# Bouncing two mixer outputs through DRAM: smaller pieces, another order, and residual rows on GpSimd's queue

## The reference, cut to what matters

```python
z = _rms_norm(h, norm_mix_g)
p = z @ w_in                                  # [conv value | conv gate | S5 input], 512 channels each
conv_out = silu(_layer_norm(conv31(conv_v * sigmoid(conv_gate)) + conv_b))
y = s5_forward(ssm_u) + s5_backward(ssm_u) + d_skip * ssm_u
y = gelu(y)
ssm_out = y * sigmoid(y @ glu_w + glu_b)
h = h + concat(conv_out, ssm_out) @ w_out     # 1024 x 1024
z = _rms_norm(h, norm_ffn_g)
h = h + square(relu(z @ w_ff1)) @ w_ff2       # 1024 -> 4096 -> 1024
out = _rms_norm(h, norm_final_g)
```

## Time and profile before

| | us |
|---|---|
| three runs of the kernel | 924.2, 924.34, 1046.33 |
| median | 924.34 |
| the profiled execution, its own time | 924.33 |
| its span on the slowest core (core 0) | 923.3 |
| spans of the eight cores | 917.6 to 923.3 |
| mean granted TensorE clock of the cores | 0.945 to 0.953 |

### The profile page before, as it was taken

How to read it: one execution, slowest core, us unless ns; L and a number is a source line. 1 busy time by engine, 2 the same in 40 slices (tenths; PEclk the granted TensorE clock), 3 DMA queues, 4 the chain that set the end, 5 groups by cost and what they waited for, 6 DMA issues and landing times.

```text
span 923.3 us, 15660 instructions; the slowest of 8 cores (917.6 to 923.3 us)
## 1 busy us (share of the span) xinstructions
PE 777.3 (84%) x4515; PEld 388.4 (42%) x4584; DVE 497.0 (54%) x955; ACT 367.6 (40%) x596; POOL 400.2 (43%) x454
## 2 busy tenths in 40 slices
PE   0466667598886996689999999999999999999992
PEld 0233334246344565235544444444444444444440
DVE  5647971847878845426643343343343343343487
ACT  5878976534124455636632112111111111111453
POOL 3777991864879816000043323324333333323220
PEclk9978888799998999879999999999999999999997
DMA  8469974561449885699041410606023060510134
GB/s 229 149 201 241 168 183 81 94 99 33 66 79 103 75 129 154 181 229 262 6 60 33 65 28 2 91 1 92 1 38 55 1 92 1 70 22 1 46 137 182
DMA packets 71955, 87.27 MB, mean 95 GB/s; under 512 B 7584, under 2 KB 55840, under 8 KB 71872
## 3 DMA queue, kind: packets, MB, share of 16 engines
q1 hardware_dynamic: 56752, 66.18, 30.8%
q0 software_dynamic: 14400, 19.76, 14.3%
q10 hardware_dynamic: 720, 0.33, 0.1%
HBM read 86.56 MB, written 19.45 MB: 115 GB/s over the span
## 4 chain that ended last, share of the span: by engine, by line
PE 66%; DVE 8%; issue 8%; ACT 7%; DMA 5%; SPq 3%; POOL 2%; DVEq 0%; ACTq 0%; POOLq 0%
PE p_pb L1142 24%; PE p_pb L1162 23%; PE p_pb L1088 6%; SPq L162 3%; PE p_pb L1011 3%; DVE p_pb L477 2%; PE p_pb L448 2%; ACT s_zt L349 2%; DMA scr_uc<-s_usc 2%; DMA s_xt<-xl 2%; PE p_pb L691 1%; PE p_pb L930 1%; ACT s_wb L640 1%; DVE s_vo L477 1%; PE p_pb L941 1%
## 5 line engine op out<-in xcount | busy, mean ns | idle before, releaser
L477 DVE TENSOR_TENSOR s_h<-s_h,p_pb 128x512 f32<-128x512 f32 x288 | 197.7, 687 | 262.2 <-PE p_pb L1162 246.6
L477 POOL TENSOR_TENSOR s_hid<-s_rl 128x512 bf16<-128x512 f32 x128 | 133.7, 1049 | 322.8 <-ACT s_rl L1150 308.3
L1162 PE MATMUL p_pb<-s_w2c,s_hid 128*128 128x512 bf16 x1005 | 225.7, 379 | 5.1 <-DVE s_h L477 4.1
L1142 PE MATMUL p_pb<-s_zf,s_w1c 128*128 128x512 bf16 x1002 | 224.9, 379 | 1.2
L1150 ACT ACTIVATE s_rl<-p_pb 128x512 f32<-128x512 f32 x128 | 76.1, 597 | 327.7 <-PE p_pb L1142 315.4
L1162 PEld LDWEIGHTS p_pb<-s_w2c,s_hid 128*128 128x128 bf16 x1024 | 99.4, 98 | 126.5 <-issue 7.9
L1142 PEld LDWEIGHTS p_pb<-s_zf,s_w1c 128*128 128x128 bf16 x1024 | 100.2, 98 | 120.0
L448 PE MATMUL p_pb<-s_zsl,s_winu 128*128 128x512 bf16 x243 | 72.1, 447 | 11.6 <-ACT s_ust L462 9.2
L372 PE MATMUL p_pb<-s_ident,s_zt 128*128 128x128 bf16 (+1 forms) x264 | 24.7, 249 | 45.3 <-ACT s_zt L358 34.7
L842 PE MATMUL p_pb<-s_zsl,s_winv 128*128 128x512 bf16 x250 | 55.6, 379 | 5.5 <-DVE s_usc L858 3.8
L448 PEld LDWEIGHTS p_pb<-s_zsl,s_winu 128*128 128x128 bf16 x256 | 27.2, 112 | 44.7 <-issue 28.2
(11 more groups left out here) (168 smaller groups left out, 940.2 us busy)
## 6 DMA issues: line engine op xcount, KB each, us to landing
s_xt<-xl SPq DMA_DIRECT2D x32, 512.0 KB, 6.1
s_h<-xl SPq DMA_DIRECT2D x16, 512.0 KB, 17.5
s_w1c<-w_ff POOLq DMA_DIRECT2D x8, 1024.0 KB, 9.9
s_w2c<-w_ff POOLq DMA_DIRECT2D x8, 1024.0 KB, 10.5
out<-s_h SPq DMA_DIRECT2D x15, 512.0 KB, 2.6
s_wstv<-w_in SPq DMA_DIRECT2D x4, 1024.0 KB, 8.9
s_kf<-scr_rs SPq DMA_DIRECT2D x8, 384.0 KB, 18.6
s_wstu<-w_in SPq DMA_DIRECT2D x4, 512.0 KB, 10.9
```

Of the source, the lines that this page charges most:

```text
L477: op(eng, lambda e: e.tensor_tensor(o, a, b_, op=o_), r=r, w=w)
L1142: op("pe", lambda e, k=k, f=f: e.matmul(pb[pi_][:, :], w1c[fc % 2][:, k, f * 128:(f + 1) * 128], zf[:, k, b * 512:(b + 1) * 512], start=(k ...
L1162: op("pe", lambda e, f=f, half=half: e.matmul(pb[pi_][:, :], hid[hb][:, f, ti * 128:(ti + 1) * 128], w2c[fc % 2][:, f, half * 512:(half + ...
```

## The change

Three edits. (1) The state space part is written and read per call of `ssm_out`: `ys_write(i)` writes four groups (256 KB) in each of eight calls, and `ys_read(i)` reads them with four DMAs of 64 KB. In `ys_out(i)` the reads of piece i - 1 are issued before the write of piece i. `gs` has eight keys in place of four. (2) The convolution part goes by pairs of channel chunks, and lies in the scratch in the order in which it is read: `yc_write(j)` writes 16 groups with eight DMAs, one per time residue (16 partitions x 16 rows of 512 bytes, 128 KB each, 1 MB together), and `yc_read(c)` reads a chunk with one DMA (128 partitions x 4 KB, 512 KB). (3) `resid_load` is on GpSimd's queue.

```diff
-    def back_write(name, src, skey, c):
-
-        P.dma("sp", bass.AP(scr[name], c * 128 * 2048, [[256, 128], [128 * 256, 8], [1, 256]]), src[:, 8 * c:8 * c + 8, :],
-              r=[skey], w=["scr_%s%d" % (name, c)])
-
-    def back_read(name, c, dst, dkey):
-        for gl in range(8):
-            P.dma("sp", dst[16 * gl:16 * gl + 16, c, :].rearrange("p (t k) -> p t k", t=8),
-                  bass.AP(scr[name], c * 128 * 2048 + gl * 128 * 256, [[256, 16], [16 * 256, 8], [1, 256]]),
-                  r=["scr_%s%d" % (name, c)], w=["%s_%d" % (dkey, gl)])
+    def ys_write(i):
+
+        P.dma("sp", bass.AP(scr["ys"], 4 * i * 128 * 256, [[256, 128], [128 * 256, 4], [1, 256]]), gs[:, 4 * i:4 * i + 4, :],
+              r=["gs%d" % i], w=["scr_ys%d" % i])
+
+    def ys_read(i):
+        c = i // 2
+        for gl in range(4 * (i % 2), 4 * (i % 2) + 4):
+            P.dma("sp", mixs[16 * gl:16 * gl + 16, c, :].rearrange("p (t k) -> p t k", t=8),
+                  bass.AP(scr["ys"], (8 * c + gl) * 128 * 256, [[256, 16], [16 * 256, 8], [1, 256]]),
+                  r=["scr_ys%d" % i], w=["mixs%d_%d" % (c, gl)])
+
+    def yc_write(j):
+
+        for t in range(8):
+            P.dma("sp", bass.AP(scr["yc"], 16 * j * 16 * 2048 + 256 * t, [[2048, 16], [16 * 2048, 16], [1, 256]]),
+                  sil[16 * t:16 * t + 16, 16 * j:16 * j + 16, :], r=["sil%d" % (2 * j), "sil%d" % (2 * j + 1)], w=["scr_yc%d_%d" % (j, t)])
+
+    def yc_read(c):
+        P.dma("sp", mixc[:, c, :], bass.AP(scr["yc"], c * 128 * 2048, [[2048, 128], [1, 2048]]),
+              r=["scr_yc%d_%d" % (c // 2, t) for t in range(8)], w=["mixc%d" % c])
...
     def resid_load(t):
-        P.dma("sp", h[:, t, :], _rows(xl, 2 + 128 * (t % 2), t // 2), w=["h%d" % t])
+        P.dma("pool", h[:, t, :], _rows(xl, 2 + 128 * (t % 2), t // 2), w=["h%d" % t])
...
     def ys_out(i, banks):
         ssm_out(2 * i, banks, stk)
-        if i % 2 == 1:
-            c = i // 2
-            back_write("ys", gs, "gs%d" % c, c)
-            if c > 0:
-                back_read("ys", c - 1, mixs, "mixs%d" % (c - 1))
+        if i > 0:
+            ys_read(i - 1)
+        ys_write(i)
...
     def yc_out(c):
         for i in range(4 * c, 4 * c + 4):
             ln_silu(i)
-        back_write("yc", sil, "sil%d" % c, c)
-        if c > 0:
-            back_read("yc", c - 1, mixc, "mixc%d" % (c - 1))
+        if c % 2 == 1:
+            yc_write(c // 2)
+            yc_read(c - 1)
+            yc_read(c)
 
     for i in range(8):
         ys_out(i, (0, 1) if i % 2 == 0 else (6, 7))
-    back_read("ys", 3, mixs, "mixs3")
+    ys_read(7)
     for c in range(4):
         yc_out(c)
-    back_read("yc", 3, mixc, "mixc3")
```

More of the change, by code:

```diff
@@ L983, in ln_silu @@
         op("act", lambda e: e.activation(sil[:, 2 * i:2 * i + 2, :], yv[:, 2 * i:2 * i + 2, :], AF.Silu), r=["yv%d" % i], w=["sil%d" % (i // 4)])
-    def back_write(name, src, skey, c):
-        P.dma("sp", bass.AP(scr[name], c * 128 * 2048, [[256, 128], [128 * 256, 8], [1, 256]]), src[:, 8 * c:8 * c + 8, :],
-              r=[skey], w=["scr_%s%d" % (name, c)])
-    def back_read(name, c, dst, dkey):
-        for gl in range(8):
-            P.dma("sp", dst[16 * gl:16 * gl + 16, c, :].rearrange("p (t k) -> p t k", t=8),
-                  bass.AP(scr[name], c * 128 * 2048 + gl * 128 * 256, [[256, 16], [16 * 256, 8], [1, 256]]),
-                  r=["scr_%s%d" % (name, c)], w=["%s_%d" % (dkey, gl)])
+    def ys_write(i):
[14 more added lines that the diff above has]
+              r=["scr_yc%d_%d" % (c // 2, t) for t in range(8)], w=["mixc%d" % c])
     for c in range(4):
         for gl in range(8):
-            P.place("mixc%d_%d" % (c, gl), "mixc", WIN + 8192 + 4096 * c, 4096, 16 * gl, 16 * gl + 16)
+            P.place("mixc%d" % c, "mixc", WIN + 8192 + 4096 * c, 4096)
             P.place("mixs%d_%d" % (c, gl), "mixs", WB2 + 4096 * c, 4096, 16 * gl, 16 * gl + 16)
     gs = at("gs", [128, 32, 256], BF16, VV1)
-    for c in range(4):
-        P.place("gs%d" % c, "gs", VV1 + 4096 * c, 4096)
+    for i in range(8):
+        P.place("gs%d" % i, "gs", VV1 + 2048 * i, 2048)
     def ssm_out(pp0, banks, stk):
@@ L1039, in ssm_out @@
             op("act", lambda e, g0=g0, bi=bi: e.activation(gs[:, g0:g0 + 3:2, :], pb[bi][:].rearrange("p (g k) -> p g k", g=2), AF.Gelu_apprx_tanh),
-               r=[pbk[bi]], w=["gs%d" % (pp0 // 4)])
+               r=[pbk[bi]], w=["gs%d" % (pp0 // 2)])
     gluw = sb("gluw", [128, 4, 512], BF16, UST)
@@ L1045, in _build @@
     msk = [["mixs%d_%d" % (c, gl) for gl in range(8)] for c in range(4)]
-    mck = [["mixc%d_%d" % (c, gl) for gl in range(8)] for c in range(4)]
+    mck = [["mixc%d" % c] for c in range(4)]
     def glu_mm(b, banks):
@@ L1490, in _build @@
         resid_load(t)
-    P.dma("pool", w1c[0][:], w1v[:, :, 0:512], r=["mixc3_7"], w=["w1c0"])
+    P.dma("pool", w1c[0][:], w1v[:, :, 0:512], r=["mixc3"], w=["w1c0"])
     P.dma("pool", w2c[0][:], w2v[0], w=["w2c0"])
```

## The result

The ratio of the changed kernel to the one before is 1.0172, with a 95% interval of 1.0117 to 1.0227. On the 924.34 us of before that is 940.2; the forecast was 938. The ratio leaves out disturbed executions, which the plain medians of that comparison, 942.17 and 937.82, hold. So the kernel is slower; whether by more than 2% the interval leaves open. The profiled execution after took 940.96.

A forecast was written before the change was run, and what follows sets the result against it. SP's in-order DMA queue was taken to bound the stretch where TensorE waits for mixs and mixc. State space +12.9 and convolution with loads +1.6 gave 14.5, taken as 13.7 on 924.33: 938 us, range 927 to 946.

The forecast's parts named there:

- Part 2: Convolution part, 16 issues fewer but two landings in series: 20.7 us in place of 26.4, gaining 5.7 us alone.
- eight writes at 0.5 us: Convolution part, first eight writes on SP's queue: last issued at 3.5, landed at 6.2 us after SP is free.
- Part 1, the step: State space part, per piece on SP's queue: landing 2.7, wake-up 0.15, four reads 2.35, together 5.2 us; loss +12.9 us.
- the four reads at 4 x 0.59: State space part, SP's issue of one piece's four reads of mixs: 2.35 us of each step.
- The wake-up of 0.15: State space part, time from a write's landing to the first read's issue on SP's queue: 0.15 us.
- The GELU spacing: State space part: a GELU pair every 3.1 to 3.3 us, so SP falls behind from the second piece on.
- Part 1, the first write: State space part, first ys write beside the wout and gluw loads: 2.7 + 1.3 = 4.0 us, landed 344.7.
- Part 3: Residual loads on GpSimd's queue compete with the convolution part's DMAs: cost 7.3 us, turning -5.7 into +1.6.
- Sum: Whole kernel: 12.9 + 1.6 = 14.5 us, taken as 13.7 because some h loads start later than the reads; 938 us.
- Rival 1: Residual loads on GpSimd's queue don't disturb: +12.9 - 5.7 = +7.2, 931.5 us; chance 0.22.
- Rival 2: State space round trips longer: step 6 us, +18, and +2 for the rest, 944 us; over 943, chance 0.2.
- Rival 3: State space part keeps pace with the GELUs (step under 3.3 us): -2 to -9, about 918 us; chance 0.08.

The follow-up runs named there:

- e2: Only the convolution part's edit (pairs of chunks, row order) on the kernel before, residual loads still on SP's queue; ratio 0.9981, a gain of 1.8 us.
- e1: Only the state space part's edit (pieces of four groups, reads of piece i-1 before write i) on the kernel before; ratio 1.0105, 9.8 us slower.
- e4: Changed kernel with the write of piece i issued ahead of the reads of piece i-1 in the state space part; 1.001 of the kernel before.
- e3: Only the residual loads moved to GpSimd's queue, on the kernel before; ratio 1.0219, 20.3 us slower.
- e5: Changed kernel with the residual loads back on SP's queue; 1.0096 of the kernel before.
- e7: From e6, the eight writes of a pair in residue order 0, 1, 4, 5, 2, 3, 6, 7; 0.995 of the kernel before.
- e6: From e5, state space write ahead of the previous piece's reads, and all sixteen convolution writes ahead of the four reads; 0.9959 of the kernel before.
- e10: From e7, reads of the first pair issued after the fourth write of the second pair; 0.9958 of the kernel before.
- e9: From the kernel before, each residual load on GpSimd's queue moves a 1 KB quarter of the rows of four tiles; ratio 1.0311, last landing 429.0.

## Why the prediction was right or wrong, and which terms were off

The direction, the order of the writes as the main loss and the price of part 3 came out as forecast. The step that failed is the sum of part 2. That the total still came near is luck: two errors of opposite sign.

**Part 2, the step that failed.** "So the part alone gains 5.7 us"; measured by itself it gains 1.8. The term mis-sized most is "eight writes at 0.5 us", the last landed 6.2 after the start. In e2 the first read went out 8.6 us after the first write, and in the changed kernel, 384.03 to 393.03, 9.0. The 0.5 is the issue of a write of 512 KB from 128 partitions (two in 1.00 us); these are 128 KB from 16 partitions and keep SP 0.7 to 0.8 us each with nothing beside them. What holds them stays open. The last reads landed 5.9 us after their issue, where the sum had 4.8. That sum also has allowances that it doesn't name: 7.3 + 7.2 is given as 15.2, and 15.9 + 3.6 (1.05 MB at 290 GB/s) as 20.7.

**Part 1, the step.** Right in kind: shown by e1 and by the swap in e4. The step was forecast at 5.2 us and measured 4.75. Landing was 2.7 (median of the eight writes), as taken. The term that was too large is the four reads at 4 x 0.59: they take 1.72. The 0.59 was a mean over groups of eight and sixteen (0.74, 0.57 and 0.52); groups of four took 0.43 each in seven of eight cases. The wake-up of 0.15 was read from a gap between two issues that waited for nothing; it is too small to matter. The GELU spacing named with the earlier trace rows is 3.05 us there and 3.5 for the pair before it, not 3.1 to 3.3, and nothing hangs on that either.

**Part 1, the first write.** It failed on the other side. "Half of that excess for half the bytes" gave 4.0 us; it took 9.0. In the earlier trace rows the first write took 5.8 and in the changed kernel 9.0, yet both landed at about 348. The last of the two weight loads on GpSimd's queue landed at 346.4 before and at 348.4 after. That the write waited for their traffic is read from this, and from what the queues moved in the changed kernel from 339.5 to 348.7 us, four times as much on GpSimd's; no run moves those loads:

```profile
q0 software_dynamic: 799, 1.05, 74.6%
q1 hardware_dynamic: 528, 0.26, 12.8%
```

So issuing the write earlier gained nothing. The two errors cancelled: SP was free at 383.8 (forecast 383.6), the GLU got going at 386.06 (forecast 385.7). Alone, part 1 cost 9.8 us and not 12.9.

**Part 3.** Forecast +7.3 beside part 2; measured 7.0 beside parts 1 and 2 and 4.2 beside part 2 alone. So the size is right here. Where it falls is not: the prediction put 4.5 us on the stretch with h0 and h1 (15.2 to 19.7) and 2.8 on the last two reads, which were to share with h2 and on. The traces have about 5.0 on the first and nothing on the last reads (5.83 us against 5.92). Even shares also fail elsewhere: against the 64 KB reads with rows of 512 bytes the same loads cost 20.3 us (e3), where I had expected 2 to 8. The rule that the prediction weighed, of the Trainium skill, "DMA: Bandwidth & Descriptors", section "Issuing engines are not separate DMA queues", says that the queues interleave on the same DMA engines. The traces agree in that loads on GpSimd's queue held up SP's transfers; how unevenly they can share it doesn't say. Whether a second queue brings bandwidth isn't settled here: the prediction took 249 and 253 GB/s as equal, but e3 moved 333 with both.

**Sum.** 12.9 + 1.6 = 14.5, taken as 13.7; measured 1.72% = 15.9 us. By the single measurements it is 9.8 - 1.8 + 7.0 = 15.0: part 1 was put 3.1 us too high, the gain of part 2 3.9 us too high, and only because the two nearly cancel is the total close. Rival 1 (loads don't disturb) is refuted by e5, which is faster than the changed kernel and has 10.2 us where that has 15.2. Rival 2 (a step of 6 us) is out with a step of 4.75. Rival 3 (SP keeps pace) came true only with the order swapped, and then without its gain: e4 has the GLU early, but a convolution part of 31.6 us, where the rival had 28.

## What to carry to other kernels

In a queue that is worked off in order, issue the write that is ready ahead of the read that must wait for an earlier landing; the reverse puts every round trip in series (4.75 us for each of the pieces here). That smaller pieces then make it worse follows from this, but no run has large pieces in that order. Moving a bulk load that nobody waits for to an idle engine's queue can cost much: its place behind the urgent DMAs on the same queue had kept it out of their way. When several edits touch one resource, measure them alone and in pairs: here one edit cost 20 us alone and 4 beside another that by itself gained 2.

The best version found is e7: small pieces with the write first, row-ordered convolution part with all writes ahead of the reads, loads left on SP: 0.995 of the kernel before (0.9931 to 0.9969). It isn't told apart from e6 and e10.

## What I had not expected of the hardware

Two queues, both with work waiting, got very unequal shares: in e3 4.17 MB against 0.83 in 15 us, in e9 2.83 against 0.34 in 12. And pieces of 512 or 1024 bytes on GpSimd's queue came out as packets of 3.3 and 3.7 KB (2.7 KB with each piece a DMA of its own), so in these runs the row length in the access pattern did not set the packet size there. Last, two loads of 512 KB on that queue delayed eight writes with rows of 512 bytes by 5 us, while 14 of them issued just behind two reads with rows of 4 KB delayed those by nothing.
